# The expert sum of a two-block forward pass: another order on VectorE, and the gates stored in the order of their reader

## Chip, cores, metric

One Trainium2 chip, one core. The metric is the device time of one execution in microseconds, as the median of several. The engines are TensorE (PE), VectorE (DVE), ScalarE (ACT), GpSimd (POOL) and SyncE (SP); each runs its own list of instructions in order and waits on semaphores. Sixteen DMA engines serve the queues of SP (q1), ACT (q10) and POOL (q0).

## The reference, cut to what matters

A forward pass of 512 tokens of width 1024 through two blocks. The change touches the expert layer of the first block. Each token picks 128 of 16,384 single-neuron experts with 128 gates; its output is the gated sum of their value rows:

```
act = jnp.einsum('td,ted->te', x_blk, u[i_blk]).astype(f32)
hid = jax.nn.gelu(act, approximate=False) * g_blk
return jnp.einsum('te,ted->td', hid.astype(v.dtype), v[i_blk])
```

All is float32 outside; the kernel splits each operand into two bf16 parts (hi and lo) and adds three products.

## The kernel before

The kernel doesn't gather rows of `u` and `v` for most tokens. It computes the activations of all experts for all tokens, spreads each token's gates over all experts (zero where not chosen), multiplies, and multiplies by all of `v`.

**The expert stage** (`C_U`, 64 chunks). A chunk is 256 experts, 1 MB of `u`. For each of its two halves (t = 0, 1) PE fills a bank of PSUM, ACT's `gelu_tile` writes it to `u_st[c % 2]`, and POOL's `store_activations` stores the pair to `act_dram`; the gelu of two chunks later waits for that store (`u_stored`). In the second half of the stage (i = 4 to 7, from about 730 us) the kernel also builds the gates of tokens 128 to 511: DVE writes one-hot tiles (L1907, L1912), PE multiplies them, and ACT copies the result to `g_st` (L1350), 48 tokens for each of two buffers b. Every four chunks POOL stores one buffer to `gate_dram` (`store_gates`, L574), seven in all, each as one block of 24 KB in every partition. The eighth stays in `g_st[:, 1]`. `g_stored[b]` says that a buffer is free again.

**The value stage** (`C_V`, 64 chunks of 256 experts, 1 MB of `v` each). Per chunk c:

- ACT issues two loads (`load_experts`): activations of 384 tokens (L468) and the gates of the chunk, out of all seven groups (L470), two chunks ahead, into one of two buffers.
- DVE multiplies them (L1922 twice, L1924) to `h_f` and signals `h_mul`. ACT casts `h_f` to `h_hi` (L1357), DVE subtracts to `h_lo` (L1926). PE needs it for `values(c)`, 36 matmuls into six banks that accumulate over the whole stage.
- For the weights three chunks ahead ACT makes `w_hi` (L1314, in `hi_in_loop`), when PE has finished the chunk that used the slot (`v_done`), and DVE `w_lo` (L1826, in `lo_in_loop`). SP refills a slot of the ring of four after `w_lo`.
- Block 0 (tokens 0 to 127) goes another way: POOL gathers for each token its activation (`load_act`, L593) and its value row (`load_value`, L597), one slot of 128 at a time, and DVE adds the weighted row to `res` (L1936), two slots a chunk. Eight rows are in flight; a new one is gathered when a row has been added (`fma_done`).

DVE's order within a chunk is: products, h_lo, w_lo, two row adds. ACT's is: wait for the products, issue the loads of chunk c+2, h_hi, w_hi. Gathers of the second block (L624) fetch 64 rows each, those of L593 and L597 128.

After the stage ACT's `norm` begins with block 0, once all 128 row adds are done, and goes on with the other blocks out of PSUM.

Of the kernel before, what the change touches and what calls it, by code (L numbers as in the profile page):

```python
# [7 lines left out]
F32 = mybir.dt.float32  # L8
# [3 lines left out]
ALU = mybir.AluOpType  # L12
ACT = mybir.ActivationFunctionType
AX_X = mybir.AxisListType.X

P = 128
# [19 lines left out]
PH, PK, PTOP = 8, 128, 16  # L36
PE_N = PK * PK
SLOTS = PH * PTOP
# [10 lines left out]
RING = 4  # L49
AHEAD = 3  # L50
# [5 lines left out]
N_U = PK // 2  # L56
N_V = PK // 2
# [12 lines left out]
C_U = C_QUERY + N_QUERY  # L70
C_V = C_U + N_U
# [26 lines left out]
TD = T - P  # L98
GT = TD // 8
ATS = TD // 32  # L100
ROWS = 8
# [25 lines left out]
def build_program(nc, w_all, x_in, cols_in, small_in, rows_in, out):  # L127
    ctx = ExitStack()
    with ctx:
# [10 lines left out]
        res = sb("res", [P, TB, D])  # L140
# [22 lines left out]
        ps = ctx.enter_context(nc.psum_tensor("ps", [P, 8, 512], F32))  # L163
# [51 lines left out]
        g_st = view(0, 2, PK, GT)  # L215
# [35 lines left out]
        tok_f = sb("tok_f", [P, TB])  # L251
        zero_i = sb("zero_i", [P, 2], I32)
        act_dram = nc.dram_tensor("act_dram", (N_U, P, 2 * T), F32, kind="Internal").ap()
        gate_dram = nc.dram_tensor("gate_dram", (7, P, PK, GT), F32, kind="Internal").ap()


        c_hi = view(0, KT, T, dt=BF16)
# [208 lines left out]
        def load_experts(eng, i, c):  # L466
            n = i * 8 + c
            eng.dma_start(ga_in[:, c % 2, :, :], act_dram[n].rearrange("p (j t) -> p j t", j=2)[:, :, P:T]).then_inc(h_ld[c % 2], 16)  # L468
            pairs = gate_dram.rearrange("g p (n j) t -> n p g (j t)", j=2)
            eng.dma_start(g_in[:, c % 2, :, :, :].rearrange("p g j t -> p g (j t)"), pairs[n]).then_inc(h_ld[c % 2], 16)  # L470

        block = ctx.enter_context(nc.Block())

# [47 lines left out]
        def _(pool):  # L521
# [49 lines left out]
                    store_activations(i, c)  # L571
            def store_gates(i, b):
                pool.wait_ge(g_out, 4 + 2 * (ATS * (i - 4) + 6 * b + 6))
                pool.dma_start(gate_dram[(i - 4) * 2 + b], g_st[:, b, :, :]).then_inc(g_stored[b], 16)  # L574

            with pool.Fori(4, 7) as i:
                for c in range(8):
# [5 lines left out]
                if c == 3:  # L583
                    store_gates(7, 0)

            pool.wait_ge(slot_done, 1)
            for r in range(2):
                pool.wait_ge(u_stored[r], 16 * (N_U // 2 + 1))
            acts = act_dram.rearrange("n p (t o) -> (n p t) o", o=1)
            values_in = w_all.rearrange("n p (j d) -> (n p j) d", j=2)  # L590

# [4 lines left out]
            def load_value(k):  # L596
                pool.indirect_dma_start(v_rows[k % ROWS], None, values_in,  # L597
                                        bass.IndirectOffsetOnAxis(ap=v_idx[:, k:k + 1], axis=0)).then_inc(row_in[k % ROWS], 16)

            for k in range(ROWS):  # L600
                load_act(k)
            for k in range(ROWS):
                load_value(k)
            for k in range(ROWS, 2 * ROWS):
                load_act(k)
# [559 lines left out]
        def _(act):  # L1165
# [143 lines left out]
            def hi_in_loop(c, arrived, done, count):  # L1309

                s = (c + AHEAD) % RING
                act.wait_ge(w_ld[s], arrived)
                act.wait_ge(done, count)
                act.activation(w_hi[:, s, :], w_st[:, s, :], ACT.Copy).then_inc(w_hi_done, 1)  # L1314

            def gelu_tile(i, c, t):
                if t == 0:
                    act.wait_ge(u_stored[c % 2], 16 * (4 * i + c // 2 + 1))
                act.wait_ge(u_done, 16 * i + 2 * c + t + 3)
                act.activation(u_st[:, c % 2, t, :], ps[:, t, :], ACT.Gelu).then_inc(u_out, 1)  # L1320
# [12 lines left out]
                    act.activation(gate_t, gate_t, ACT.Exp).then_inc(soft_e, 1)  # L1333
                experts(TB - 1, c)
            act.drain().then_inc(g_out, 4)
            with act.Fori(4, 8) as i:
                for c in range(8):
                    hi_in_loop(c, 16 * (C_U // RING + 2 * i + (c + AHEAD) // RING + 1), u_done, 16 * i + 2 * c + 2)
                    for t in range(2):
                        gelu_tile(i, c, t)  # L1340
                        if t and c % 2:
                            continue
                        at = 2 * c + t - c // 2
                        b, first = at // 6, (at % 6) * 8
                        if at % 6 == 0:
                            act.wait_ge(g_stored[b], 16 * (i - 3))
                        for bank in range(2):
                            act.wait_ge(g_done, 2 * (ATS * (i - 4) + at) + bank + 5)
                            tok = slice(first + bank * 4, first + bank * 4 + 4)
                            act.activation(g_st[:, b, :, tok].rearrange("p k t -> p t k"),  # L1350
                                           ps[:, 2 + 2 * (at % 2) + bank, :].rearrange("p (t k) -> p t k", t=4), ACT.Copy).then_inc(g_out, 1)
            def expert_values(i, c):
                act.wait_ge(h_mul, 8 * i + (c + 1))
                if not isinstance(i, int) or c + 2 < 8:
# [2 lines left out]
                act.activation(h_hi[:, c % 2, :, :], h_f[:, c % 2, :, :], ACT.Copy).then_inc(h_hi_done, 1)  # L1357
                hi_in_loop(c, 16 * (C_V // RING + 2 * i + ((c + AHEAD) // RING + 1)), v_done, 8 * i + (c + 2))

            act.wait_ge(g_stored[0], 16 * 5)  # L1360
            act.wait_ge(g_stored[1], 16 * 4)
            for c in range(2):
                load_experts(act, 0, c)
            for r in range(2):
                act.wait_ge(u_stored[r], 16 * (N_U // 2 + 1))
            with act.Fori(0, N_V // 8 - 1) as i:
                for c in range(8):
                    expert_values(i, c)
# [69 lines left out]
            for u, (h, qb) in enumerate(UNITS):  # L1438
                n = (qb + 1) * P
# [129 lines left out]
        def _(dve):  # L1569
# [252 lines left out]
            def lo_in_loop(c, n):  # L1822

                s = (c + AHEAD) % RING
                dve.wait_ge(w_hi_done, n + 1)
                dve.tensor_tensor(w_lo[:, s, :], w_st[:, s, :], w_hi[:, s, :], ALU.subtract).then_inc(w_lo_done, 1)  # L1826
# [89 lines left out]
            out_0 = res[:, 0, :]  # L1916
            with dve.Fori(0, N_V // 8) as i:
                for c in range(8):
                    dve.wait_ge(h_ld[c % 2], 32 * (4 * i + (c // 2 + 1)))
                    for j in range(2):  # L1920
                        by_group = lambda v: v[:, 0:7 * GT].rearrange("p (g t) -> p g t", g=7)
                        dve.tensor_tensor(by_group(h_f[:, c % 2, j, :]), by_group(ga_in[:, c % 2, j, :]), g_in[:, c % 2, :, j, :], ALU.mult)  # L1922
                    last_t = slice(7 * GT, TD)
                    dve.tensor_tensor(h_f[:, c % 2, :, last_t], ga_in[:, c % 2, :, last_t], g_st[:, 1, bass.ds(16 * i + 2 * c, 2), :], ALU.mult).then_inc(h_mul, 1)  # L1924
                    dve.wait_ge(h_hi_done, 8 * i + (c + 1))
                    dve.tensor_tensor(h_lo[:, c % 2, :, :], h_f[:, c % 2, :, :], h_hi[:, c % 2, :, :], ALU.subtract).then_inc(h_lo_done, 1)  # L1926
                    lo_in_loop(c, C_V + 8 * i + c + AHEAD)
                    b = c // 4
                    if c % 4 == 0:
                        dve.wait_ge(act_ld[b], 16 * ROWS * (i + 1))  # L1930
                        at = bass.ds(2 * ROWS * i + b * ROWS, ROWS)
                        dve.tensor_tensor(gh[:, b, :], act_0[:, at], gate_0[:, at], ALU.mult)
                    for r in range(2 * (c % 4), 2 * (c % 4) + 2):
                        dve.drain()
                        dve.wait_ge(row_in[r], 16 * (2 * i + (b + 1)))
                        dve.scalar_tensor_tensor(out_0, v_rows[r], gh[:, b, r:r + 1], out_0, ALU.mult, ALU.add).then_inc(fma_done, 1)  # L1936
            split[0] = C_CONV + AHEAD

            for t in range(TB + 1):
# [403 lines left out]
```

## Time and profile before

| | |
|---|---|
| median of 3 runs | 3003.16 us (2999.53 to 3011.18) |
| the profiled execution | 3000.2 us, span 2998.6 us |
| busy over the span | PE 89%, DVE 68%, ACT 43%, POOL 19% |
| value stage | from about 1113 to 1776 us |

Times in rows are microseconds from the span's start. "Busy" leaves out waits and the issuing of DMAs. The granted clock of PE is 1.00 at 2.4 GHz and 0.50 at 1.2 GHz.

### The profile page before, as it was taken

The page shows a single profiled execution, that of the slowest core. Times are in us where ns is not written, and L with a number is a line of the kernel's source. Part 1 is how long each engine was busy: PE and PEld are TensorE (multiplying, and loading weights), DVE is VectorE, ACT ScalarE, POOL GpSimd, SP SyncE. Part 2 cuts the span into 40 slices and gives each one's busy share as a digit, 9 for nine tenths or more (in the row PEclk, how much of TensorE's full clock was granted, in tenths as well). Part 3 has the DMA queues.
Part 4 walks back from the last instruction along what each step waited for, and adds up shares of the span by engine and source line. Part 5 has one row for each costly group of instructions (what it writes and reads, how often), then busy time and mean ns, then how long its engine had stood idle before and what let it go on. Part 6 is the DMA issues. An engine that isn't in the chain of part 4 may idle for free. (4 is left out here: it accounts for less than half of the span.)

```text
span 2998.6 us, 39872 instructions
## 1 busy us (share of the span) xinstructions
PE 2666.7 (89%) x14118; PEld 1340.6 (45%) x14323; DVE 2027.9 (68%) x3310; ACT 1293.9 (43%) x1379; POOL 555.5 (19%) x480
## 2 busy tenths in 40 slices
PE   6988999999999987777777769999999889999994
PEld 3464444444555543333333334445554445555552
DVE  4545688885788756666666664436653579899895
ACT  4333223323444432222222233344443368887884
POOL 0000000000000027455454400000000233222221
PEclk9988999999999998999999989999999889999997
DMA  4301333344455458888888842222112389999994
GB/s 183 113 15 64 113 134 136 144 147 162 181 218 206 179 198 294 272 279 280 273 279 276 278 152 87 101 83 71 57 57 99 141 306 400 395 398 397 395 397 166
DMA packets 173835, 609.03 MB, mean 203 GB/s; under 512 B 74672, under 2 KB 91056, under 8 KB 123184
## 3 DMA queue, kind: packets, MB, share of 16 engines
q1 hardware_dynamic: 57312, 411.62, 36.7%
q0 software_dynamic: 40656, 149.00, 14.0%
q10 hardware_dynamic: 75776, 47.19, 5.5%
q8 instruction: 58, 0.95, 0.1%
q14 instruction: 33, 0.27, 0.0%
HBM read 539.59 MB, written 68.16 MB: 203 GB/s over the span
## 5 line engine op out<-in xcount | busy, mean ns | idle before, releaser
L683 PE MATMUL ps<-w_hi,arena 128*128 128x512 bf16 (+1 forms) x1583 | 605.6, 383 | 133.6 <-DVE arena L1926 107.7
L684 PE MATMUL ps<-w_lo,arena 128*128 128x512 bf16 (+1 forms) x1582 | 604.1, 382 | 38.7 <-DVE arena L1926 38.6
L684 PE MATMUL ps<-a_lo,w_hi 128*128 128x512 bf16 x1654 | 628.6, 380 | 6.3 <-DVE a_lo L1602 1.8
L685 PE MATMUL ps<-a_hi,w_lo 128*128 128x512 bf16 x1653 | 628.0, 380 | 1.4
L683 PE MATMUL ps<-a_hi,w_hi 128*128 128x512 bf16 x1604 | 609.9, 380 | 2.5 <-ACT arena L1411 0.7
L685 PE MATMUL ps<-w_hi,arena 128*128 128x512 bf16 (+1 forms) x1583 | 604.1, 382 | 1.0
L1826 DVE TENSOR_TENSOR w_lo<-w_st,w_hi 128x2048 bf16<-128x2048 f32 x128 | 293.2, 2291 | 177.8 <-ACT w_hi L1314 166.1
L683 PEld LDWEIGHTS ps<-w_hi,arena 128*128 128x128 bf16 (+1 forms) x1600 | 166.6, 104 | 374.0 <-DVE arena L1926 163.7
L1357 ACT ACTIVATE arena<-arena 128x768 bf16<-128x768 f32 x64 | 53.9, 842 | 494.6 <-issue 352.9
L1320 ACT ACTIVATE xn<-ps 128x512 f32<-128x512 f32 x128 | 76.5, 598 | 428.1 <-PE ps L685 428.1
L1578 DVE TENSOR_TENSOR w_lo<-w_st,w_hi 128x2048 bf16<-128x2048 f32 x67 | 153.1, 2289 | 152.9 <-ACT w_hi L1174 152.7
L685 PEld LDWEIGHTS ps<-a_hi,w_lo 128*128 128x128 bf16 x1680 | 164.7, 98 | 199.6 <-issue 2.5
L683 PEld LDWEIGHTS ps<-a_hi,w_hi 128*128 128x128 bf16 x1680 | 164.9, 98 | 190.7 <-issue 4.6
L685 PEld LDWEIGHTS ps<-w_hi,arena 128*128 128x128 bf16 (+1 forms) x1600 | 166.9, 104 | 182.4 <-issue 5.2
L684 PEld LDWEIGHTS ps<-a_lo,w_hi 128*128 128x128 bf16 x1680 | 164.8, 98 | 183.0 <-issue 1.7
L1314 ACT ACTIVATE w_hi<-w_st 128x2048 bf16<-128x2048 f32 x128 | 243.3, 1901 | 3.0 <-issue 2.4
L684 PEld LDWEIGHTS ps<-w_lo,arena 128*128 128x128 bf16 (+1 forms) x1600 | 166.9, 104 | 170.9 <-issue 4.3
L567 POOL DMA_DIRECT2D act_dram<-xn x64 | 34.1, 533 | 770.6 <-ACT xn L1320 760.1
L1912 DVE TENSOR_SCALAR xn<-iota_b,arena 128x128 bf16<-128x128 bf16 x768 | 175.7, 313 | 0.0
L1174 ACT ACTIVATE w_hi<-w_st 128x2048 bf16<-128x2048 f32 x67 | 127.2, 1903 | 105.9 <-PE ps L685 105.9
L2104 DVE TENSOR_TENSOR w_lo<-w_st,w_hi 128x2048 bf16<-128x2048 f32 x64 | 146.0, 2282 | 28.0 <-ACT w_hi L1497 28.0
L593 POOL DMA_INDIRECT arena<-act_dram,h_idx x128 | 155.6, 1215 | 44.8 <-issue 39.6
(392 smaller groups left out, 3858.7 us busy)
## 6 DMA issues: line engine op xcount, KB each, us to landing
w_st<-in_w_all SPq DMA_DIRECT2D x260, 1024.0 KB
arena<-in_w_all SPq DMA_DIRECT2D x64, 1024.0 KB
act_dram<-xn POOLq DMA_DIRECT2D x64, 512.0 KB, 2.9
xn<-in_w_all SPq DMA_DIRECT2D x32, 1024.0 KB, 9.2
arena<-act_dram ACTq DMA_DIRECT2D x64, 384.0 KB
gate_dram<-arena POOLq DMA_DIRECT2D x7, 3072.0 KB, 11.7
arena<-gate_dram ACTq DMA_DIRECT2D x64, 336.0 KB
a_hi<-in_w_all SPq DMA_DIRECT2D x16, 1024.0 KB, 9.1
```

Source lines behind the costliest of these rows:

```text
L593: pool.indirect_dma_start(act_0[:, k:k + 1], None, acts, bass.IndirectOffsetOnAxis(ap=h_idx[:, k:k + 1], axis=0)).then_inc(act_ld[k // ROW ...
L683: pe.matmul(dst, l_hi, r_hi, start=start, stop=False)
L684: pe.matmul(dst, l_hi, r_lo, start=False, stop=False)
L685: return pe.matmul(dst, l_lo, r_hi, start=False, stop=stop)
L1174: act.activation(dst, w_st[:, n % RING, :], ACT.Copy).then_inc(w_hi_done, 1)
L1314: act.activation(w_hi[:, s, :], w_st[:, s, :], ACT.Copy).then_inc(w_hi_done, 1)
L1320: act.activation(u_st[:, c % 2, t, :], ps[:, t, :], ACT.Gelu).then_inc(u_out, 1)
L1357: act.activation(h_hi[:, c % 2, :, :], h_f[:, c % 2, :, :], ACT.Copy).then_inc(h_hi_done, 1)
L1578: dve.tensor_tensor(lo_n, w_st[:, n % RING, :], hi_n, ALU.subtract).then_inc(w_lo_done, 1)
L1826: dve.tensor_tensor(w_lo[:, s, :], w_st[:, s, :], w_hi[:, s, :], ALU.subtract).then_inc(w_lo_done, 1)
L1912: last = dve.tensor_scalar(oh_a[:, at % 2, r, part, :], iota_b[:, :], c_slot[:, 0, k:k + 1], c_slot[:, 2 + part, k:k + 1], ALU.is_equal, A ...
L2104: dve.tensor_tensor(w_lo[:, s, :], moe_st[k % MOE_RING], w_hi[:, s, :], ALU.subtract).then_inc(w_lo_done, 1)
```

## The change

1. Layout of `gate_dram`: from (group, partition, expert tile, token) to (chunk, partition, group, two tiles x 48 tokens). A store of one group writes 64 pieces of 384 bytes in each partition; a load of one chunk reads one piece of 2688 bytes in each partition. Before, a store wrote one piece of 24,576 bytes in each partition and a load read seven of 384 bytes.
2. DVE's order in the value stage: h_lo(c), the products of chunk c+1, two row adds, w_lo last. The row adds start with chunk 4, four chunks later than before, and the last eight follow the last chunk.
3. ACT issues the loads of the first two chunks within the last part of the expert stage, after chunk 6 of i = 7. Its wait for the last activation stores comes before the value loop, as before.
4. POOL issues the first four value-row gathers before it waits for the last activation stores.

```diff
-        gate_dram = nc.dram_tensor("gate_dram", (7, P, PK, GT), F32, kind="Internal").ap()
+        gate_dram = nc.dram_tensor("gate_dram", (N_V, P, 7, 2 * GT), F32, kind="Internal").ap()
...
-            pairs = gate_dram.rearrange("g p (n j) t -> n p g (j t)", j=2)
-            eng.dma_start(g_in[:, c % 2, :, :, :].rearrange("p g j t -> p g (j t)"), pairs[n]).then_inc(h_ld[c % 2], 16)
+            eng.dma_start(g_in[:, c % 2, :, :, :].rearrange("p g j t -> p (g j t)"), gate_dram[n].rearrange("p g x -> p (g x)")).then_inc(h_ld[c % 2], 16)
...
-                pool.dma_start(gate_dram[(i - 4) * 2 + b], g_st[:, b, :, :]).then_inc(g_stored[b], 16)
+                by_group = gate_dram.rearrange("n p g x -> g p n x")
+                pool.dma_start(by_group[(i - 4) * 2 + b], g_st[:, b, :, :].rearrange("p (n j) t -> p n (j t)", j=2)).then_inc(g_stored[b], 16)
...
+            pool.wait_ge(slot_done, 1)
+            for k in range(4):
+                load_value(k)
+            for r in range(2):
+                pool.wait_ge(u_stored[r], 16 * (N_U // 2 + 1))
             for k in range(ROWS):
                 load_act(k)
-            for k in range(ROWS):
+            for k in range(4, ROWS):
                 load_value(k)
...
+            for c in range(8):
+                experts_and_gates(7, c)
+                if c == 6:
+                    act.wait_ge(g_stored[0], 16 * 5)
+                    act.wait_ge(g_stored[1], 16 * 4)
+                    for n in range(2):
+                        load_experts(act, 0, n)
+            for r in range(2):
+                act.wait_ge(u_stored[r], 16 * (N_U // 2 + 1))
...
+            def expert_values(i, c, rows=True, more=True):
+                dve.wait_ge(h_hi_done, 8 * i + (c + 1))
+                dve.tensor_tensor(h_lo[:, c % 2, :, :], h_f[:, c % 2, :, :], h_hi[:, c % 2, :, :], ALU.subtract).then_inc(h_lo_done, 1)
+                if more:
+                    products(i, c + 1)
+                if rows:
+                    b, batch = (c // 4 + 1) % 2, 2 * i + (c // 4 - 1)
+                    if c % 4 == 0:
+                        weigh(b, i + c // 4, 2 * ROWS * i + (c // 4 - 1) * ROWS)
+                    for r in range(2 * (c % 4), 2 * (c % 4) + 2):
+                        add_row(b, r, batch)
+                lo_in_loop(c, C_V + 8 * i + c + AHEAD)
+
+            products(0, 0)
+            for c in range(8):
+                expert_values(0, c, rows=c >= 4)
+            with dve.Fori(1, N_V // 8 - 1) as i:
                 for c in range(8):
...
+                    expert_values(i, c)
+            for c in range(8):
+                expert_values(N_V // 8 - 1, c, more=c < 7)
+            weigh(1, N_V // 8, SLOTS - ROWS)
+            for r in range(ROWS):
+                add_row(1, r, SLOTS // ROWS - 1)
```

`products`, `weigh` and `add_row` hold the same instructions as the old loop.

## Rows read from the trace of the kernel before

**Rows 1.** Busy time by stretch: PE, PEld, DVE, ACT, POOL; clock, DMA share, GB/s.
```profile
1128.00:1138.50 10.50, 5.20 (x13) 1.89 (x14) 7.14 (x8) 2.64 (x2) 8.67 (x7) 0.51 0.96 326
...
1180.00:1700.00 520.00, 399.63 (x1794) 174.86 (x1831) 346.99 (x368) 134.82 (x102) 260.80 (x204) 1.00 0.85 277
...
2500.00:2900.00 400.00, 389.56 (x2273) 202.56 (x2272) 355.16 (x213) 328.42 (x261) 114.35 (x70) 1.00 1.01 396
```

**Rows 2.** Timeline of PE, one chunk: start, us, line, tiles, [idle before <-releaser].
```profile
1300.01 0.39 PE L683 MATMUL ps<-w_hi,arena 128*128 128x512 bf16 x1 [2.40 <-DVE arena L1926]
...
1307.58 0.38 PE L685 MATMUL ps<-w_hi,arena 128*128 128x512 bf16 x1
1310.20 0.39 PE L683 MATMUL ps<-w_hi,arena 128*128 128x512 bf16 x1 [2.24 <-DVE arena L1926]
```

**Rows 3.** Timeline of DVE, the same chunk.
```profile
1300.80 2.29 DVE L1826 TENSOR_TENSOR w_lo<-w_st,w_hi 128x2048 bf16<-128x2048 f32 x1 [0.84 <-ACT w_hi L1314]
1303.18 2.66 DVE L1936 SCALAR_TENSOR_TENSOR res<-arena,res 128x1024 f32<-128x1024 f32 x2
1305.76 0.92 DVE L1922 TENSOR_TENSOR arena<-arena 128x336 f32<-128x336 f32 x2
...
1309.18 0.96 DVE L1926 TENSOR_TENSOR arena<-arena 128x768 bf16<-128x768 f32 x1 [2.33 <-ACT arena L1357]
```

**Rows 4.** Timeline of ACT, the same chunk; ACTq is the issuing of a DMA.
```profile
1307.05 0.56 ACTq L468 DMA_DIRECT2D arena<-act_dram  x1
1307.76 0.50 ACTq L470 DMA_DIRECT2D arena<-gate_dram  x1
1308.31 0.84 ACT L1357 ACTIVATE arena<-arena 128x768 bf16<-128x768 f32 x1 [7.54 <-issue]
1309.06 1.89 ACT L1314 ACTIVATE w_hi<-w_st 128x2048 bf16<-128x2048 f32 x1
```

**Rows 5.** DMA queues from 1200 to 1700 us: packets, MB, share of 16 engines.
```profile
q0 software_dynamic: 17147, 51.06, 30.7%
q1 hardware_dynamic: 7056, 51.38, 29.0%
q10 hardware_dynamic: 57414, 35.90, 25.1%
```

**Rows 6.** Timeline around the start of the value stage, three engines.
```profile
1102.18 0.62 ACTq L470 DMA_DIRECT2D arena<-gate_dram  x1
...
1106.74 0.59 PE L937 MATMUL ps<-res,ident 128*128 128x512 f32 x1
...
1108.19 0.93 DVE L1922 TENSOR_TENSOR arena<-arena 128x336 f32<-128x336 f32 x2 [12.63 <-DMA arena<-gate_dram]
...
1113.08 0.63 PE L684 MATMUL ps<-w_lo,arena 128*128 128x512 bf16 x1 [5.74 <-DVE arena L1926]
```

**Rows 7.** Timeline around the end of the value stage.
```profile
1773.75 1.06 ACT L1184 ACTIVATE xn<-res 128x1024 f32<-128x1024 f32 x1 [5.11 <-DVE res L1936]
...
1775.52 0.38 PE L685 MATMUL ps<-w_hi,arena 128*128 128x512 bf16 x1
```

**Rows 8.** Timeline of the expert stage: the first gate store, and the gelu of three chunks later.
```profile
775.65 0.53 POOL L574 DMA_DIRECT2D gate_dram<-arena  x1 [0.20 <-issue]
...
802.25 0.60 ACT L1320 ACTIVATE xn<-ps 128x512 f32<-128x512 f32 x1 [2.78 <-PE ps L685]
```

**Rows 9.** DMA issues: count, KB each, median us from issue to landing.
```profile
act_dram<-xn POOLq DMA_DIRECT2D x64, 512.0 KB, 2.9
...
gate_dram<-arena POOLq DMA_DIRECT2D x7, 3072.0 KB, 11.7
```

**Rows 10.** Single lines on POOL: duration in ns, min/median/max, first and last start.
```profile
L567 POOL DMA_DIRECT2D act_dram<-xn x64: 533/533/544, 396.8 to 1102.2; - x64
...
L593 POOL DMA_INDIRECT arena<-act_dram,h_idx x128: 942/1015/2828, 1107.9 to 1698.7; - x128
...
L624 POOL DMA_INDIRECT arena<-x_dram,arena x32: 912/2782/3372, 2409.3 to 2902.0; - x32
```

More of the change, by code:

```diff
@@ L584, in _ @@
                     store_gates(7, 0)
-            pool.wait_ge(slot_done, 1)
-            for r in range(2):
-                pool.wait_ge(u_stored[r], 16 * (N_U // 2 + 1))
             acts = act_dram.rearrange("n p (t o) -> (n p t) o", o=1)
@@ L1335, in _, with experts_and_gates @@
             act.drain().then_inc(g_out, 4)
-            with act.Fori(4, 8) as i:
-                for c in range(8):
[L1338 to L1351, printed above, removed]
+            def experts_and_gates(i, c):
+                hi_in_loop(c, 16 * (C_U // RING + 2 * i + (c + AHEAD) // RING + 1), u_done, 16 * i + 2 * c + 2)
+                for t in range(2):
+                    gelu_tile(i, c, t)
+                    if t and c % 2:
+                        continue
+                    at = 2 * c + t - c // 2
+                    b, first = at // 6, (at % 6) * 8
+                    if at % 6 == 0:
+                        act.wait_ge(g_stored[b], 16 * (i - 3))
+                    for bank in range(2):
+                        act.wait_ge(g_done, 2 * (ATS * (i - 4) + at) + bank + 5)
+                        tok = slice(first + bank * 4, first + bank * 4 + 4)
+                        act.activation(g_st[:, b, :, tok].rearrange("p k t -> p t k"),
+                                       ps[:, 2 + 2 * (at % 2) + bank, :].rearrange("p (t k) -> p t k", t=4), ACT.Copy).then_inc(g_out, 1)
@@ new lines, in _ @@
+            with act.Fori(4, 7) as i:
+                for c in range(8):
+                    experts_and_gates(i, c)
+            for c in range(8):
[7 more added lines that the diff above has]
+                act.wait_ge(u_stored[r], 16 * (N_U // 2 + 1))
@@ L1358, in expert_values @@
                 hi_in_loop(c, 16 * (C_V // RING + 2 * i + ((c + AHEAD) // RING + 1)), v_done, 8 * i + (c + 2))
[L1360 to L1365, printed above, removed]
             with act.Fori(0, N_V // 8 - 1) as i:
@@ L1915, in _ @@
             dve.wait_ge(g_out, 4 + 2 * TD // 8)
-            out_0 = res[:, 0, :]
-            with dve.Fori(0, N_V // 8) as i:
-                for c in range(8):
[L1919 to L1936, printed above, removed]
@@ new lines, in products @@
+            def products(i, c):
+                dve.wait_ge(h_ld[c % 2], 32 * (4 * i + (c // 2 + 1)))
+                for j in range(2):
+                    by_group = lambda v: v[:, 0:7 * GT].rearrange("p (g t) -> p g t", g=7)
+                    dve.tensor_tensor(by_group(h_f[:, c % 2, j, :]), by_group(ga_in[:, c % 2, j, :]), g_in[:, c % 2, :, j, :], ALU.mult)
+                last_t = slice(7 * GT, TD)
+                dve.tensor_tensor(h_f[:, c % 2, :, last_t], ga_in[:, c % 2, :, last_t], g_st[:, 1, bass.ds(16 * i + 2 * c, 2), :], ALU.mult).then_inc(h_mul, 1)
@@ new lines, in weigh, with add_row @@
+            def weigh(b, count, at):
+                dve.wait_ge(act_ld[b], 16 * ROWS * count)
+                at = bass.ds(at, ROWS)
+                dve.tensor_tensor(gh[:, b, :], act_0[:, at], gate_0[:, at], ALU.mult)
+            def add_row(b, r, batch):
+                dve.drain()
+                dve.wait_ge(row_in[r], 16 * (batch + 1))
+                dve.scalar_tensor_tensor(res[:, 0, :], v_rows[r], gh[:, b, r:r + 1], res[:, 0, :], ALU.mult, ALU.add).then_inc(fma_done, 1)
+            def expert_values(i, c, rows=True, more=True):
[10 more added lines that the diff above has]
+                lo_in_loop(c, C_V + 8 * i + c + AHEAD)
```

## The prediction

> **What bounds the kernel now.** I read the page's slices first: the only long stretch in which TensorE is not nearly full lies at about 1110 to 1780 us, the value stage. The table of stretches shows it in numbers [rows 1]: from 1180 to 1700 TensorE is busy 399.6 of 520 us, DVE 347.0, ACT 134.8, GpSimd 260.8, and the DMA engines 0.85 of the time. No engine is full, so a loop of waits sets the pace. The timeline of one chunk shows it. TensorE's 36 matmuls run from 1300.01 to 1307.80 (35 spacings of 0.216 us, and one more), 7.79 us, then nothing until 1310.20, when h_lo has come from DVE [rows 2]. The period is 10.19 us. Backwards from there: w_lo starts at 1300.80, the two row adds at 1303.18, the products at 1305.76, and h_lo only at 1309.18 [rows 3]. Between them ACT issues two loads from 1307.05, and then does h_hi at 1308.31 and w_hi at 1309.06 [rows 4]; w_lo of the next chunk needs that w_hi. So the ring is w_lo 2.38, adds 2.58, products and handover 1.29, two issues 1.26, h_hi 0.75, w_hi 1.92 to the next w_lo: 10.18 us. All but h_hi and w_hi hang on each other only by the order in which DVE was told to work.
>
> **The change, part by part.**
>
> *Order on DVE.* After h_lo(c) come the products of chunk c+1, then two row adds (now four chunks behind), and w_lo(c+3) last. Nothing is added or removed: DVE's elapsed work stays 2.38 + 2.58 + 1.29 + 0.96 = 7.21 us, about 7.3 with handovers. Call E the end of values(c-1). ACT may do w_hi(c+3) from E + 0.2 to E + 2.1, the two issues to E + 3.5, h_hi(c+1) to E + 4.4. DVE does w_lo(c+3) from E + 2.1 to E + 4.4 and h_lo(c+1) to E + 5.4; TensorE wants it at E + 7.8. It has 2.4 us to spare. DVE then does products and adds to E + 9.3 and waits for w_hi at E + 9.9: 0.6 us of slack. The ring is open and TensorE's 7.79 us is the floor.
>
> *What is late next: the DMA engines.* The three queues use 30.7 + 29.0 + 25.1 = 84.8% of 16 engines [rows 5], 8.65 us per chunk and engine, for 277 GB/s x 10.19 = 2.82 MB. The gate load is today 896 pieces of 384 B (seven groups by 128 partitions), afterwards 128 of 2688 B. Its price from the same rows: q1 moves 51.38 MB in 0.290 x 8000 = 2320 engine-us, 22.1 GB/s. At that rate the 12,544 activation pieces (49 chunks x 256, 1536 B, 69 ns) take 870 of q10's 2008 engine-us, and 1138 are left for 43,904 gate pieces: 26 ns each. 6272 pieces of 2688 B at 22.1 GB/s are 762. Saved: 376 / (49 x 16) = 0.48 us per chunk, leaving 8.17. Bounds of the period: 7.79 (transfers hidden; the last stage draws 396 GB/s, at which 2.82 MB need 7.1 us) and 8.17 (a share of 1.00). In the one stretch of this stage that is full, 1128 to 1138.5, a share of 0.96 went with 326 GB/s [rows 1], which is nearer the upper bound. I take 8.05 us.
>
> *Stage length.* The first matmul is at 1112.7 (one slow spacing before the first recorded, 1113.08 [rows 6]), the last ends at 1775.7 [rows 7]: 663.0 us for 64 chunks, 10.8 over 64 x 10.19, much of it at half clock (0.51 in 1128 to 1138.5 [rows 1]). How much of that stays can't be seen; none to all, I take half, 5.4. New stage: 64 x 8.05 + 5.4 = 520.6, a gain of 142.4.
>
> *Start.* The first loads are issued a chunk early, before ACT's last w_hi of the stage before. They cost ACT four issues, 2.6 us by [rows 4]; the gelu behind them slips by about 1, and TensorE is then still in the other half of the chunk. Today DVE waits for them until 1108.19 and TensorE until 1113.08, after its preload of PSUM ended at 1107.3 [rows 6]. Afterwards the products are done before, and 1107.3 + h_hi 0.84 + h_lo 0.96 + handovers 0.4 = 1109.5: gain 3.2. The four row loads that GpSimd now issues before its wait for the last activation store take time in which it waited anyway.
>
> *End.* The adds lag by a batch, so eight stand behind the last w_lo. That one is done about 3.4 before TensorE's end T; eight adds of 1.33 end at T + 7.3. Today ACT begins block 0's norm, first in its order, at 1773.75, which is T - 2.0 [rows 7]. Loss 9.3 us.
>
> *Stores.* Each of seven gate stores turns from 128 pieces of 24,576 B into 8192 of 384 B. They pass through GpSimd's queue, where the activation store of the next chunk stands behind them. Their cover: a gate store issued at 775.65 is followed by a store at +10.5, and the gelu that needs that buffer runs at 802.25, at +26.6 [rows 8]. A store lands 2.9 us after issue [rows 9], so GpSimd and the queue may be held G = 23.7 us before anything slips. Data: 8192/16 = 512 pieces per engine x 26 ns = 13.3 us, against 11.7 to landing now [rows 9]. The Trainium skill, "DMA: Bandwidth & Descriptors", Specifications, says a transfer below 512 B is done as read-modify-write; if that doubled a piece it would be 27 us, 3 us of slip a store and some 20 in all; no row here has a small store to agree or not. GpSimd's own work per piece: bounded above by charging all 533 ns of a 128-row store to its rows, 4.2 ns, 34 us a store; below by the gathers, whose shortest took 942 ns for 128 rows and 912 for 64 [rows 10], 0.5 ns a row, 4 us. I take the lower half, since rows hardly count there: no slip at 4 to 24 us, and 1.3 us in all for stray ones.
>
> *Sum.* 142.4 + 3.2 - 9.3 - 1.3 = 135.0 us. The profiled run took 3000.2 (span 2998.6), giving 2865.2; the median of the three runs, 3003.16, stands 3.0 above it (0.1%), and I add half: 2867.
>
> **Rivals.**
>
> *Loads late (B).* The gate load of chunk c+2 is now issued at E(c-2) + 2.8 and wanted at E(c-1) + 5.4, a period and 2.6 us later, where it had nearly two of 10.2. With DVE's 0.6 us of slack, a landing time L sets a period of L - 3.2. The first gate load, issued at 1102.18, was waited for until 1108.19, 6 us, on quieter queues [rows 6]. So 8.05 stands up to L = 11.2. At L = 12 the period is 8.8: 663.0 - 563.2 - 10.8 + 3.2 - 9.3 = 83, so 2918. At L = 13.4 the period is back at 10.2 and nothing is gained (D): about 3005.
>
> *Stores hold GpSimd mildly (C1).* At 4.2 ns a piece each store slips 34 - 23.7 = 10.7 us, 75 over seven: 2942.
>
> *The other side (C2): stores hold it for long.* Same place, steeper: the slip is 7 x (G - 23.7). It eats all 136 at G = 43 us, 5.3 ns a piece, not far over the upper bound; at 8 ns (G = 66) the gelus, and TensorE behind their PSUM, lose 296, and the time is about 3160. What speaks for it: DVE is busy while these stores are issued, and single gathers took 2828 ns instead of 942 [rows 10]. Against it: the direct stores stayed between 533 and 544 ns. The Trainium skill, "SBUF — State Buffer", section "SBUF: two separate sides", says that GpSimd can't write descriptors while a VectorE 2-port operation holds the shared port; by that rule G would stretch with DVE's load. The gathers' spread agrees with it, the constant 533 ns neither way.
>
> **How the numbers follow.** A (ring opens, 7.8 to 8.4 us a chunk) 0.60; its own range runs from 7.79 and no cold loss (gain 158, 2843) to 8.4, all of it and 5 for the stores (gain 104, 2898). B 0.16 (2898 to 2935), C1 0.10 (2898 to 2990), C2 0.09 (mostly above 3018), D 0.05 (within 0.5%). Range 2840 to 2930 holds A, most of B and a third of C1: 0.80. Faster by over 0.5% (15 us, about what a measurement of this kernel tells from no change): 0.86; within 0.05; slower 0.09.
>
> **What would show it.** In the profile after: chunk starts 8.0 us apart; TensorE's idle before L683 by DVE gone; DVE's remaining idle before w_lo, by ACT w_hi; DMA share 0.95 to 1.02 at about 350 GB/s; the under-512 B packets on GpSimd's queue instead of ACT's; chunk length in 730 to 1100 unchanged (a gate store every 46.8 us); ACT's first norm 7 us after TensorE's last value matmul. It is wrong if DVE waits for loads before the products, or if GpSimd's stores stretch and gelu waits for a store.

## Result, and the profile after

The changed kernel takes 2842.81 us (median of four runs, 2841.96 to 2843.32) against 3003.69 of the kernel before (median of four runs, 2999.53 to 3011.18). The ratio is 0.9461, 95% interval 0.9443 to 0.948. The forecast was 2867 us, with a range from 2840 to 2930. The profiled execution took 2843.14 us (span 2841.5), so 157.1 us of the span are gone; the forecast's sum was 135.0.

The value stage by stretches, after (same columns as [rows 1]):

```profile
1110.00:1609.00 499.00, 494.75 (x2256) 225.36 (x2304) 424.72 (x457) 168.35 (x127) 406.84 (x251) 1.00 0.98 358
1200.00:1550.00 350.00, 348.21 (x1589) 158.62 (x1622) 304.36 (x329) 119.62 (x90) 293.70 (x181) 1.00 1.00 365
```

TensorE is busy 348.2 of 350 us; [rows 1] had 399.6 of 520. The DMA engines stand at a share of 1.00, moving 365 GB/s instead of 277. The half-clock stretch of [rows 1] is gone: the granted clock is 1.00 for the whole stage.

One chunk on DVE, after, which answers to [rows 3]:

```profile
1298.83 2.29 DVE L1834 TENSOR_TENSOR w_lo<-w_st,w_hi 128x2048 bf16<-128x2048 f32 x1 [0.70 <-ACT w_hi L1316]
1301.04 0.95 DVE L1945 TENSOR_TENSOR arena<-arena 128x768 bf16<-128x768 f32 x1
1301.91 0.92 DVE L1929 TENSOR_TENSOR arena<-arena 128x336 f32<-128x336 f32 x2
...
1303.09 2.66 DVE L1941 SCALAR_TENSOR_TENSOR res<-arena,res 128x1024 f32<-128x1024 f32 x2
1306.60 2.29 DVE L1834 TENSOR_TENSOR w_lo<-w_st,w_hi 128x2048 bf16<-128x2048 f32 x1 [0.85 <-issue]
```

And on ACT, which answers to [rows 4]:

```profile
1296.89 1.91 ACT L1316 ACTIVATE w_hi<-w_st 128x2048 bf16<-128x2048 f32 x1 [4.58 <-PE ps L687]
1297.07 0.56 ACTq L468 DMA_DIRECT2D arena<-act_dram  x1
1297.89 0.46 ACTq L469 DMA_DIRECT2D arena<-gate_dram  x1
1298.70 0.83 ACT L1371 ACTIVATE arena<-arena 128x768 bf16<-128x768 f32 x1
1304.66 1.91 ACT L1316 ACTIVATE w_hi<-w_st 128x2048 bf16<-128x2048 f32 x1 [5.13 <-PE ps L687]
```

The distance from one w_hi, and from one w_lo, to the next is 7.77 us, which is TensorE's 36 x 0.216 us. DVE's idle time in the chunk is 0.70 to 0.85 us ahead of w_lo, and next to nothing elsewhere, and the wait of 2.24 to 2.40 us on TensorE's line [rows 2] has no successor. The w_hi starts when TensorE has left the slot, so the ring runs through TensorE. One thing differs from the forecast's timetable: ACT's two loads go out beside w_hi, at 1297.07 and 1297.89, and not after it.

The longest waits from 1200 to 1550 us confirm it (us in total, times, longest). ACT waits for TensorE; DVE's waits for w_hi are short and never over 0.9 us, and no wait of TensorE is listed:

```profile
ACT w_hi L1316 <- PE ps L687: 228.9, 45, 5.1
...
DVE w_lo L1834 <- issue: 22.8, 27, 0.9
DVE w_lo L1834 <- ACT w_hi L1316: 14.6, 19, 0.9
```

The queues over the same 350 us, which answer to [rows 5]:

```profile
q0 software_dynamic: 15854, 47.28, 35.7%
q1 hardware_dynamic: 6481, 47.19, 35.5%
q10 hardware_dynamic: 18835, 33.38, 28.4%
```

The first gate store on GpSimd's timeline, which answers to [rows 8]:

```profile
776.53 2.80 POOL L574 DMA_DIRECT2D gate_dram<-arena  x1 [0.23 <-issue]
787.05 0.54 POOL L566 DMA_DIRECT2D act_dram<-xn  x1 [7.72 <-ACT xn L1322]
```

All seven by their line (ns min/median/max, first and last start):

```profile
L574 POOL DMA_DIRECT2D gate_dram<-arena x7: 2774/2783/2796, 776.5 to 1056.9; - x7
```

And the median time to landing, from 730 to 1060 us, which answers to [rows 9]:

```profile
gate_dram<-arena POOLq DMA_DIRECT2D x7, 3072.0 KB, 19.3
act_dram<-xn POOLq DMA_DIRECT2D x28, 512.0 KB, 2.9
```

A gate store now holds GpSimd for 2.78 us instead of 0.53 and lands after 19.3 us instead of 11.7. The seven still come 46.7 us apart ((1056.9 - 776.5) / 6), as before, and no gelu waits for a store.

Start and end of the stage, which answer to [rows 6] and [rows 7]; the last row is the first ACT copy of the layer after the norm:

```profile
1102.12 0.60 ACT L1322 ACTIVATE xn<-ps 128x512 f32<-128x512 f32 x1 [3.60 <-PE ps L687]
...
1110.36 0.38 PE L686 MATMUL ps<-w_lo,arena 128*128 128x512 bf16 x1 [2.17 <-DVE arena L1945]
...
1607.21 0.38 PE L687 MATMUL ps<-w_hi,arena 128*128 128x512 bf16 x1
...
1609.81 5.41 DVE L1941 SCALAR_TENSOR_TENSOR res<-xn,arena,res 128x1024 f32<-128x1024 f32 x4
1615.25 1.06 ACT L1186 ACTIVATE xn<-res 128x1024 f32<-128x1024 f32 x1 [13.43 <-DVE res L1941]
...
1657.66 0.57 ACT L1409 ACTIVATE arena<-ps 128x512 f32<-128x512 f32 x1
```

Where the 157.1 us come from:

| part | before | after | gain |
|---|---|---|---|
| last gelu to first value matmul | 11.4 | 8.0 | +3.4 |
| 64 chunks | 663.0 | 497.3 (64 x 7.77) | +165.7 |
| last value matmul to the first ACT copy of the next layer | 39.2 | 50.2 | -11.0 |
| ahead of the expert stage (not touched) | | 0.9 later | -0.9 |

Of the 165.7 us, about 156 are the shorter period, 63 x (10.25 - 7.77): in the kernel before the mean of the 47 spacings between w_lo from 1200 to 1700 us is 10.25, a little over the 10.19 of the one chunk in [rows 2], and the last chunk takes only TensorE's own time in both. The other 10 or so were lost in the kernel before at the start of the stage. DVE, which had the first two row adds ahead of the products of chunk 1, waited for GpSimd's first gathers, and TensorE stood idle until it got the late h_lo. From the timeline of the kernel before:

```profile
1122.03 0.17 DVE L1932 TENSOR_TENSOR arena<-arena,gate 128x8 f32 x1 [6.28 <-DMA arena<-act_dram,h_idx]
...
1124.92 1.29 DVE L1936 SCALAR_TENSOR_TENSOR res<-arena,res 128x1024 f32<-128x1024 f32 x1 [2.73 <-DMA arena<-in_w_all,v_idx]
...
1133.31 0.61 PE L683 MATMUL ps<-w_hi,arena 128*128 128x512 bf16 x1 [10.05 <-DVE arena L1926]
```

With a third wait of 1.46 us for the second row that is 10.5 us, and h_lo of chunk 1 starts 20.6 us after that of chunk 0 (1132.29 and 1111.66), 10.4 more than a period. In the changed kernel the row adds begin with chunk 4, and TensorE has no idle time between the start of the value matmuls and 1180 us.

### The profile page after: what moved, and what is told of

It is laid out like the page before. It is cut to its first block and busy times, and to the rows that moved or that the text cites. A ratio compares the mean times of both kernels' runs of the same rounds, so it can differ in the third digit from the quotient of the medians.

```text
span 2841.5 us, 39775 instructions
## 1 busy us (share of the span) xinstructions
PE 2652.2 (93%) x14118; PEld 1344.3 (47%) x14323; DVE 2021.4 (71%) x3310; ACT 1294.2 (46%) x1379; POOL 654.1 (23%) x480
## 5 line engine op out<-in xcount | busy, mean ns | idle before, releaser
L685 PE MATMUL ps<-w_hi,arena 128*128 128x512 bf16 (+1 forms) x1583 | 602.2, 380 | 16.3 <-ACT arena L1522 14.6
L590 POOL DMA_INDIRECT arena<-act_dram,h_idx x128 | 270.6, 2114 | 39.9 <-issue 39.9
L2134 DVE TENSOR_TENSOR w_lo<-arena,w_hi 128x2048 bf16<-128x2048 f32 x64 | 144.7, 2281 | 4.2 <-ACT w_hi L1505 4.2
## 6 DMA issues: line engine op xcount, KB each, us to landing
gate_dram<-arena POOLq DMA_DIRECT2D x7, 3072.0 KB, 19.3
```

The costliest lines, as they stand in the source:

```text
L590: pool.indirect_dma_start(act_0[:, k:k + 1], None, acts, bass.IndirectOffsetOnAxis(ap=h_idx[:, k:k + 1], axis=0)).then_inc(act_ld[k // ROW ...
L685: pe.matmul(dst, l_hi, r_hi, start=start, stop=False)
L2134: dve.tensor_tensor(w_lo[:, s, :], moe_st[k % MOE_RING], w_hi[:, s, :], ALU.subtract).then_inc(w_lo_done, 1)
```

## Experiments

**The layout alone.** The kernel before with only the new shape of `gate_dram`, its load and its store:

```diff
-        gate_dram = nc.dram_tensor("gate_dram", (7, P, PK, GT), F32, kind="Internal").ap()
+        gate_dram = nc.dram_tensor("gate_dram", (N_V, P, 7, 2 * GT), F32, kind="Internal").ap()
...
```

> The kernel before, with the new gate layout alone. My theory: the ring of waits over DVE and ACT sets the period, 10.2 us a chunk, and no DMA is in it, so 0.48 us less DMA time a chunk buys nothing: 3001 us, within 5, DMA share in the value stage down from 0.85 to about 0.80. Rival: the loads were in the ring (ACT issues 896 small pieces before h_hi), and the period falls with them, to 9.7 us, 2972.

Measured: 3003.42 us beside 3000.98, ratio 1.0001 (0.999 to 1.0012), as the theory has it. The engine time does fall. From 1200 to 1550 us:

```profile
1200.00:1550.00 350.00, 267.20 (x1199) 116.99 (x1224) 233.21 (x248) 91.05 (x70) 175.79 (x139) 1.00 0.81 277
```

and on ACT's queue:

```profile
q10 hardware_dynamic: 14180, 25.13, 22.6%
```

A share of 0.81 for 277 GB/s, where [rows 1] have 0.85. With the old order no engine waits for a load in this stretch, so it is worth nothing. TensorE's idle time at the start of the stage is still there too (9.52 us before its matmul at 1137.72). The stores cost nothing either, though they take 2783 ns here too.

**The order alone.** The changed kernel with the old shape of `gate_dram`, its load and its store (the diff above, reversed).

> The changed kernel with the old gate layout: new orders on DVE, ACT and GpSimd alone. Theory 1: the DMA engines are full at 7.77 us a chunk (share 1.00 in the changed kernel), so the 0.48 us a chunk of the small pieces come back whole: 8.2 to 8.3 us a chunk, 2871 to 2877 us. Theory 2: TensorE is the only bound and a full DMA share is elastic, since the engine time a chunk had fallen from 8.65 to 7.75 where only 0.48 were taken away: 7.8 us, 2843 to 2848. Theory 3: the many small pieces make the gate loads land later than the period plus 2.6 us allow, and DVE waits before the products: over 8.6 us, above 2896.

Measured: 2843.34 us (2842.88 to 2843.49), ratio 0.9473 (0.9457 to 0.9489). That is theory 2: the whole gain is there without the layout. The same stretch:

```profile
1200.00:1550.00 350.00, 348.21 (x1590) 158.65 (x1622) 304.50 (x329) 119.50 (x90) 292.91 (x181) 1.00 1.03 365
```

and ACT's queue in it:

```profile
q10 hardware_dynamic: 53617, 33.31, 32.9%
```

TensorE is as full as in the changed kernel. q10 carries three times the packets and takes 32.9% instead of 28.4%, and one wait of 0.7 us is all that is listed for it in the 350 us. The forecast priced this kernel's DMA work at 8.65 us a chunk, which would have set the period; it ran 7.77, at a share of 1.03, which is 8.00 us of engine time. TensorE has no idle time at the start of the stage beyond the 2.2 us before its first value matmul (looked at up to 1150 us). This kernel has all the new orders; DVE's two moves (products earlier, row adds later) and GpSimd's early gathers were not tried one by one.

**Every gate store twice.** The first of the two goes to a second tensor that nobody reads; the waits count both.

```diff
+                for to in (gate_copy, gate_dram):
+                    by_group = to.rearrange("n p g x -> g p n x")
+                    pool.dma_start(by_group[(i - 4) * 2 + b], g_st[:, b, :, :].rearrange("p (n j) t -> p n (j t)", j=2)).then_inc(g_stored[b], 16)
...
```

> The changed kernel, each of the seven gate stores made twice (to a second, unused tensor too), so GpSimd issues 16,384 pieces of 384 B a time. Theory: the activation store behind them waits for the queue's data: 19.3 us to landing become about 37, against the 26.6 us at which the gelu wants its buffer; less the 2.9 us of its own, 12 to 13 us of slip a store, 85 to 90 in all, 2930. Rival 1: only GpSimd's own 2 x 2.8 us count, since the queue serves the small store beside them: no change, 2843. Rival 2: the ring of descriptors fills, and GpSimd itself is held: a POOL duration of the second store far above 2.8 us, with a slip as in the theory or more.

Measured: 2922.97 us in one run, span 79.8 above the changed kernel. GpSimd's timeline:

```profile
781.01 2.80 POOL L576 DMA_DIRECT2D gate_copy<-arena  x1 [0.23 <-issue]
800.98 2.81 POOL L576 DMA_DIRECT2D gate_dram<-arena  x1 [17.16 <-issue]
803.77 1.10 POOL L567 DMA_DIRECT2D act_dram<-xn  x2
```

and ACT's, where the gelu needs the buffer of that activation store:

```profile
822.20 0.60 ACT L1324 ACTIVATE xn<-ps 128x512 f32<-128x512 f32 x1 [17.40 <-DMA act_dram<-xn]
```

The second store begins only 19.97 us after the first, about when that one has landed (18.9 us is their median). GpSimd is held for 17.16 us; the profile shows nothing that it waits for. That is what the second rival of the expectation describes; that a ring of descriptors is full isn't shown. The next activation store goes out late, and a gelu waits 17.40 us for it. The stores now come 57.1 us apart ((1123.5 - 781.0) / 6, from that line's first and last start); 10.4 more for each of seven is 73 of the 79.8 us. So the path of the rivals C1 and C2, from GpSimd over a late activation store to a waiting gelu, is real, though GpSimd is held here and not busy with its pieces; with a single store no gelu waits. TensorE's clock also fell in the gaps: 0.53 from 819 to 826 us, 0.50 from 874 to 884.

**Twelve of 36 matmuls left out.** The product of h_lo with w_hi isn't computed, which takes TensorE's floor to 24 x 0.216 = 5.2 us.

```diff
-                            last = mm3(ps[:, 2 * tb + part, :], h_hi[:, c % 2, j, rows], h_lo[:, c % 2, j, rows],
-                                       w_hi[:, c, w], w_lo[:, c, w], False, done is not None and j == 1)
+                            dst, stop = ps[:, 2 * tb + part, :], done is not None and j == 1
+                            pe.matmul(dst, h_hi[:, c % 2, j, rows], w_hi[:, c, w], start=False, stop=False)
+                            last = pe.matmul(dst, h_hi[:, c % 2, j, rows], w_lo[:, c, w], start=False, stop=stop)
```

> The changed kernel without the product of h_lo and w_hi in the value stage: 24 matmuls a chunk, 5.2 us, so that TensorE is out of the way and the next bound shows. Theory 1: DVE's work is next, 7.2 to 7.3 us a chunk, 32 us off: 2811. Theory 2: GpSimd is next: its four gathers with their gaps fill 7.75 us a chunk in the changed kernel, almost without waiting for DVE, so the period stays at 7.7: 2840, with DVE waiting for rows. Theory 3: the DMA engines are next (share 1.00): also about 7.7 us, but with DVE waiting for loads or row gathers that are issued and not landed.

Measured: 2802.22 us in one run, less than any of the three theories had. One pair of w_lo lay 6.83 us apart, with DVE busy between them, and I took DVE for the next bound and 6.83 for the period. The next pair of runs shows that 6.83 is DVE's own pace and not the mean.

**The light kernel with either layout.** The same kernel again, and with the old layout beside it on the same chip. The first of the two expectations repeats the period of 6.83.

> The changed kernel without the product of h_lo and w_hi (24 matmuls a chunk), as measured once before: 2802 us, period 6.83 us, VectorE busy back to back, DMA share 1.03. It stands here as the partner of the next run, on the same chip. Both theories expect 2802 within 4 us.

> The same light kernel with the old layout: one gate store writes 128 pieces of 24,576 B, one chunk's load reads 896 pieces of 384 B. With TensorE's floor at 5.2 us a chunk, the pace is set by VectorE (6.83 us) or by the DMA engines. Theory 1 (the small pieces on the loads cost DMA time that was only covered by TensorE): 0.48 us of engine time a chunk more (the forecast's term) puts the period at about 7.3 us and the time at about 2832 us, and the gathers stay longer. Theory 2 (the DMA engines pack more in when asked, VectorE sets the pace): the period stays at 6.83 and the time within 4 us of its partner, so the layout is worth nothing even with TensorE out of the way.

Measured: 2803.81 us (2800.31 to 2805.12) with the new layout, 2832.65 (2832.18 to 2832.99) with the old; ratios to the kernel before 0.9327 (0.9308 to 0.9346) and 0.9427 (0.9409 to 0.9445). The layout is worth 28.8 us, or 0.45 us a chunk, once TensorE is out of the way. That is the time of theory 1. The stretch with the new layout:

```profile
1200.00:1550.00 350.00, 271.21 (x1149) 114.42 (x1171) 326.40 (x354) 134.40 (x98) 274.39 (x194) 0.96 1.03 395
```

and with the old one:

```profile
1200.00:1550.00 350.00, 261.06 (x1081) 109.13 (x1102) 309.38 (x335) 126.94 (x93) 260.50 (x184) 0.94 1.05 372
```

DVE's waits for the gates in it, new layout:

```profile
DVE arena L1930 <- DMA arena<-gate_dram: 11.9, 14, 1.2
```

Old layout:

```profile
DVE arena L1930 <- DMA arena<-gate_dram: 27.7, 27, 4.3
```

Two w_lo with 36 chunks between them, new layout:

```profile
1203.34 2.28 DVE L1835 TENSOR_TENSOR w_lo<-w_st,w_hi 128x2048 bf16<-128x2048 f32 x1
...
1460.04 2.28 DVE L1835 TENSOR_TENSOR w_lo<-w_st,w_hi 128x2048 bf16<-128x2048 f32 x1
```

Old layout:

```profile
1204.36 2.28 DVE L1835 TENSOR_TENSOR w_lo<-w_st,w_hi 128x2048 bf16<-128x2048 f32 x1
...
1478.65 2.28 DVE L1835 TENSOR_TENSOR w_lo<-w_st,w_hi 128x2048 bf16<-128x2048 f32 x1
```

Over these 36 chunks the period is 7.13 us with the new layout and 7.62 with the old. With the new layout 26 of the 36 lie 6.82 to 6.98 us apart, DVE going from one operation to the next, and the rest 7.5 to 8.2. So 7.13 is mostly DVE's own 6.83, plus 0.3 us in which it waits for loads; with the old layout the waits for loads bring it to 7.62. What the layout is worth here is shorter waits of DVE for the gates. That happens at a DMA share of 1.03 to 1.05, with 395 GB/s against 372, but whether the rate of the DMA engines or the delay of a single load makes DVE wait, the two runs don't tell apart. Both periods lie under TensorE's 7.77, which is why the order alone gave everything.

**The first loads after the loop.** ACT issues the loads of chunks 0 and 1 where the kernel before did, behind the last chunk of the expert stage; the new order stays. The partner on the same chip is the changed kernel itself, once more.

```diff
-                if c == 6:
-                    act.wait_ge(g_stored[0], 16 * 5)
-                    act.wait_ge(g_stored[1], 16 * 4)
-                    for n in range(2):
-                        load_experts(act, 0, n)
+            act.wait_ge(g_stored[0], 16 * 5)
+            act.wait_ge(g_stored[1], 16 * 4)
+            for n in range(2):
+                load_experts(act, 0, n)
```

> The changed kernel with ACT's first four loads back where they were, after the last part of the expert stage. Theory 1: the first matmul of the value stage comes 11.4 us after the last gelu, as before, instead of 8.0: 2846 us. Theory 2: besides, TensorE's longer idle time brings back the four spells at 1.2 GHz that the kernel before had between 1111 and 1180 us and the changed kernel has not: up to 11 us more, 2857. Rival: the spells came from the stalls between chunks, and do not come back: 2846.

> The changed kernel once more, beside the next three on one chip: 2843 us, within 1.

Measured: 2849.14 us (2845.78 to 2849.66) against the partner's 2842.98 (2842.24 to 2848.39); the intervals of the two ratios overlap (0.9458 to 0.9494, 0.9445 to 0.9483), so the traces have to carry it. The profiled spans are 2847.8 and 2841.8, and the last gelu begins at nearly the same time in both (1101.24 and 1101.73). DVE waits for the gates again:

```profile
1108.45 0.93 DVE L1928 TENSOR_TENSOR arena<-arena 128x336 f32<-128x336 f32 x2 [12.92 <-DMA arena<-gate_dram]
```

and the clock falls once; the stretches of the kernel with the late loads:

```profile
1111.00:1118.00 7.00, 4.63 (x11) 1.79 (x13) 5.59 (x8) 3.49 (x3) 5.78 (x5) 0.51 1.04 379
1118.00:1200.00 82.00, 81.58 (x373) 37.16 (x380) 60.79 (x70) 26.55 (x20) 60.77 (x42) 1.00 0.92 327
```

TensorE starts about 3.7 us later, and the matmuls at half clock until about 1118 us cost another 2 to 2.5 by my estimate (they take twice as long for some 5 us). The chunks from 1118 us on are as in the changed kernel. So the early loads were worth 6 us in the spans, part of it as clock: more than theory 1, less than theory 2. The later half-clock spells of the kernel before don't come back with the late start; they followed its own idle times, of 10.05, 4.05 and 3.06 us before TensorE's matmuls at 1133.31, 1155.63 and 1176.82.

**The tail.** Two kernels. In the first, DVE makes the last w_lo behind the eight row adds instead of before them; in the second the adds also follow two chunks behind instead of four.

```diff
-                lo_in_loop(c, C_V + 8 * i + c + AHEAD)
+                if more:
+                    lo_in_loop(c, C_V + 8 * i + c + AHEAD)
...
                 add_row(1, r, SLOTS // ROWS - 1)
+            lo_in_loop(7, C_CONV - 1 + AHEAD)
```

```diff
-                    b, batch = (c // 4 + 1) % 2, 2 * i + (c // 4 - 1)
...
+                    m = c - 2
+                    b, batch = (m // 4) % 2, 2 * i + m // 4
...
-            for r in range(ROWS):
+            for r in range(4, ROWS):
```

> The changed kernel with DVE's last w_lo of the value stage behind the row adds instead of before them. In the changed kernel DVE waits 1.9 us for it and spends 2.3 on it while the adds wait, and ACT's norm of block 0 begins 7.8 us after TensorE's last value matmul. Theory: the adds end 4.2 to 4.5 us sooner and everything behind them moves as much: 2838.5. Rival: the last rows are gathered too late for it, since each gather waits for the add eight slots before: DVE waits for rows, under 2 us gained.

> As the tail experiment, and the row adds two chunks behind instead of four, so that four adds stand at the end instead of eight. Theory: 5.3 us more off the end, the norm then begins before TensorE is done, and the longer spell at half clock behind it (1.3 us) goes too: 2832 to 2833. Rival: the first adds are now wanted at 1126 us, when the eight activation gathers of GpSimd are not done (about 1128), so DVE stalls once; over TensorE's 2.4 us of slack this comes back as a loss, up to 5 us: 2837.

Measured: 2844.04 us (2838.27 to 2845.2) for the first, 2836.64 (2836.07 to 2841.58) for the second, the partner at 2842.98. The norm of block 0 in the first:

```profile
1609.83 1.06 ACT L1186 ACTIVATE xn<-res 128x1024 f32<-128x1024 f32 x1 [9.28 <-DVE res L1941]
```

In the second:

```profile
1604.61 1.06 ACT L1186 ACTIVATE xn<-res 128x1024 f32<-128x1024 f32 x1 [3.71 <-DVE res L1941]
```

and the last value matmul of that one:

```profile
1606.28 0.38 PE L687 MATMUL ps<-w_hi,arena 128*128 128x512 bf16 x1
```

With the adds two chunks behind, the norm begins 1.7 us before TensorE's last value matmul, not 8.0 after it. The stall that its rival had for the first rows doesn't show: the row adds begin at 1123.72 without a wait. Even so the time is 4 us over the 2832 to 2833 of the theory. In the first kernel the norm begins 3.7 us after TensorE's end instead of 7.8, which is the step that its theory had. But single runs lay 5 to 6 us apart in both kernels, and the first one's profile (2838.27) is of its fastest run; from its median nothing can be said. Hence the second kernel once more, beside the changed one.

> The changed kernel once more, as the partner of the next run on the same chip: 2843 us.

> The same kernel as the run with the row adds two chunks behind and VectorE's last w_lo after the adds, measured before at 2836.6 with single runs between 2836 and 2842. If the shorter tail is worth what the trace shows (the norm of block 0 begins before TensorE's last matmul instead of 7.8 us after it), the median is 6 to 7 us under its partner's, 2836 to 2838. If it was scatter, the two medians lie within 2 us.

Measured: 2847.28 us (2841.53 to 2847.79), ratio 0.9468 (0.9454 to 0.9483), and 2836.92 (2836.13 to 2841.03), ratio 0.9445 (0.9432 to 0.9457). The single runs of each kernel fall into two groups: 2841.5 to 2843.4 and 2847.3 to 2848.4 for the changed one, 2836.1 to 2836.9 and 2840.9 to 2841.6 for this one. One profile of each kernel fell into each group, and the groups part ahead of everything the change touches: the clock is already 1.00 and 0.95 over the first 100 us. They differ again from 300 to 304 us, here in the changed kernel's profile with the shorter span (2841.8):

```profile
300.00:304.00 4.00, 4.00 (x20) 1.83 (x19) 2.04 (x2) 0.60 (x1) 0.00 (x0) 1.00 0.70 270
```

and in the one with the longer (2845.6):

```profile
300.00:304.00 4.00, 4.00 (x12) 1.44 (x11) 3.42 (x2) 0.69 (x1) 0.00 (x0) 0.54 0.35 111
```

In both TensorE is busy throughout these 4 us, once at full clock and once mostly at half. By the first gelu the second is 4.6 us behind (395.41 against 390.79). Why the clock differs between executions is open. Compared within a group, the version with the adds two chunks behind is 7.2 us (spans 2834.6, 2841.8) and 6.2 us (2839.4, 2845.6) below the changed kernel. It is the fastest version run here that computes everything. The first version, read the same way, has one run at 2838.3 and four at 2843.7 to 2845.2, some 3 to 4 us under the changed kernel's groups; that rests on one profile and isn't settled.

## Why the prediction was right

The forecast's likeliest case came true, at its very end: case A ran from 2843 us (7.79 us a chunk, no loss to the clock), and 2842.8 were measured. The sum was 22.1 us short against the profiled pair (2865.2 and 2843.1), nearly all of it in two terms, the period (17.9) and the loss at the start of the stage (5.4).

- *The ring.* Right. With the new orders alone the period is TensorE's, and with the layout alone it stays at 10.25. The timetable held within some 0.3 us (E is 1296.7 here): w_lo to E + 4.4, h_lo to E + 5.3 (forecast 5.4), row adds to E + 9.0 (9.3), next w_lo at E + 9.9 (9.9). One step was wrong: the two issues were put behind w_hi on ACT, and they run beside it, so h_hi ends at E + 2.8 and not 4.4. DVE isn't ready for it before E + 4.4, so it changed nothing.
- *The period.* This is the term that was mis-sized: 8.05 forecast, 7.77 measured, 0.28 x 64 = 17.9 us. The step behind it that failed is "8.65 us per chunk and engine" as an amount of work that stays the same however fast it is asked for, with 8.17 as the bound after the new layout. The order alone took 8.00 us of engine time (1.03 x 7.77) at a period of 7.77, the changed kernel 7.77 (1.00 x 7.77), and the light kernel delivered chunks every 7.13 us, at 395 GB/s, the rate that [rows 1] show for the last stage at 1.01. That row was in the forecast, with 7.1 us a chunk worked out from it; the stretch of 10.5 us at 326 GB/s was given more weight, and it lies in a stage that had just begun, where TensorE was idle or at half clock.
- *The price of small pieces.* 0.48 us a chunk, from 26 ns a piece. In engine time the layouts differ by 0.40 us a chunk at 10.19 us (shares of 0.85 and 0.81), 0.23 at 7.77 and 0.66 in the light kernels, so it isn't one fixed price. That the light kernels' periods differ by 0.49 is close to the forecast in part by luck, since what differs there is DVE's waiting. It was worth 28.8 us there and nothing here, because TensorE covers it; the ratios of the changed kernel and of the order alone overlap.
- *Cold clock.* The forecast laid much of 10.8 us to the half clock and let half of it stay, 5.4 us; none stayed. This step had the wrong mechanism: DVE's waits for GpSimd's first gathers, ahead of the products of chunk 1, alone make that chunk 10.4 us late, and the half clock from 1128 us followed TensorE's idle time. The row adds that start four chunks later take those waits away, with or without the layout. That the range had room for it ("none to all") was luck as to the cause. With the 17.9 that makes 23.3, the stage's 165.7 against 142.4.
- *Start.* 3.2 forecast, 3.4 measured. Putting the loads back cost 6 us rather than 3.2, since the clock falls too; the forecast had set that cost apart under the cold clock.
- *End.* -9.3 forecast, -11.0 measured. The norm moved from T - 2.0 to T + 7.8 (T is TensorE's end), 9.8 us. The other 1.2 lie in a run of TensorE's matmuls behind the norm, part of it at half clock: 7.1 us from 1800.79 to 1807.93 before, 8.3 from 1642.31 to 1650.63 after. The late norm isn't shown to be the cause of that, since with the adds two chunks behind it still takes 8.0 us. The version with the adds two chunks behind confirms where the 9.8 come from: its first copy of the next layer comes 10.5 us earlier (1646.72 against 1657.25). The lead is still 10.5 us at 1840, 9.0 just behind 1841, and 7.2 from 2104 us on; why it shrinks at these two places is open.
- *Stores.* Forecast 1.3 us, measured none. G came out at 19.3 us if it is taken as the time to landing, 4.4 under the 23.7 that are free; GpSimd itself is held for 2.78. GpSimd pays (2783 - 533) / 8064 = 0.28 ns a piece, below the lower bound of 0.5. The data takes 16.5 us (19.3 less 2.8, if it moves only after GpSimd is done), 32 ns a piece against the 26 assumed. The Trainium skill, "DMA: Bandwidth & Descriptors", Specifications, says that a transfer below 512 B is a read-modify-write; the trace doesn't show the doubling that the forecast worked out as 27 us. The Trainium skill, "SBUF — State Buffer", "SBUF: two separate sides", says that GpSimd can't write descriptors while a VectorE operation in a 2-port mode runs. The seven stores took 2774 to 2796 ns with DVE 81% busy from 776 to 1060 us, so no stretch shows there; the median gather of an activation rose from 1015 ns [rows 10] to 1808 in the fuller value stage, and no run tells whether the port is the reason.
- *Rivals.* B (loads late) did not occur: there is no wait of DVE for the gates from 1200 to 1550 us. It does occur in the light kernels, where DVE waits for the gates 14 and 27 times in the same 350 us. C1 and C2 need a G over 23.7; with the stores doubled they are there. C2's formula is too steep: there the gelu came 41.2 us after the first issue instead of 26.6, which makes 7 x 14.6 = 102 us where 79.8 were measured.

## What to carry to other kernels

When a loop's period is the sum of one chain through several engines and none of them is full, look for the links that exist only through one engine's order of instructions; moving those took the period here from 10.2 us to TensorE's 7.77, and the new layout was not needed for it. Look at the first chunks by themselves as well: 10.4 us were lost there to work that could wait, placed ahead of work that could not. Before an edit is credited, find the floor it lowers: with TensorE out of the way the new layout takes the period from 7.62 to 7.13, but both lay under TensorE's 7.77. And a DMA share of 0.85 was not 85% of what the engines could carry here: 277 GB/s became 365 to 395. The forecast would have done better to go by the highest rate in its rows, 396 GB/s.

## What the runs showed of the hardware

- The busy share of the DMA engines didn't scale with the rate. The new layout ran at 0.81 for 277 GB/s (10.19 us a chunk), 1.00 for 365 (7.77) and 1.03 for 395 (7.13): 8.25, 7.77 and 7.34 us of engine time for the same chunk. The old layout took 8.65 (0.85 at 277), 8.00 (1.03 at 365) and 8.00 (1.05 at 372). (With the mean period of 10.25 the two figures at 277 GB/s are 8.3 and 8.7.)
- ACT's issue of DMAs (0.56 and 0.46 us, at 1297.07 and 1297.89) ran beside an ACTIVATE of 1.91 us that began before it (at 1296.89).
- A second store of 8192 pieces of 384 B held GpSimd for 17.16 us beside its own 2.81, until about the time that the first landed; an activation store behind a single one wasn't held (issued at 787.05, 10.5 us after it, 0.54 us long).
- In the kernel before, TensorE's idle times of 5.74, 10.05, 4.05 and 3.06 us at the start of the value stage (ahead of 1113.08, 1133.31, 1155.63 and 1176.82) each went with a spell at half clock (0.50 to 0.52), and so did 6.07 us in the kernel with the late loads. Those of about 2.4 us from 1200 us on did not, nor did the 2.17 us ahead of 1110.36 in the changed kernel (all at 1.00).
